# A block with attention mixers and experts on one core: the input laid out by features as well, and the first weight column loaded in halves

## The reference

```python
def first_block(x, norm_mix, w_in, ...):
    h = rms_norm(x, norm_mix[l])          # x * rsqrt(mean(x*x) + EPS) * norm_mix
    proj = h @ w_in[l]                    # 1024 -> 2974 columns
    qkv_a, z_a, b_a, a_a, q_b, kv_b, gate_b, u_c = split_columns(proj)
    y_a = gdn_mixer(...)                  # causal conv of qkv_a, gated delta rule
    y_b = nsa_mixer(...)                  # compressed, selected and window attention
    y_c = pool_mixer(...)
    x = x + concatenate([y_a, y_b, y_c]) @ w_out[l]
    h = rms_norm(x, norm_ffn[l])
    x = x + square(relu(h @ w_ffn1[l])) @ w_ffn2[l]
```

## Time and profile before

| | |
|---|---|
| median of three runs | 1006.93 us |
| profiled execution, its time | 1007.91 us |
| profiled execution, its span from first to last instruction | 1006.1 us |
| mean granted clock of TensorE | 0.99 of 2.4 GHz |
| PE busy | 967.6 us, 96% of the span |
| DVE busy | 417.2 us, 41% |
| ACT busy | 192.1 us, 19% |
| POOL busy | 30.2 us, 3% |
| moved by DMA | 301.45 MB, 300 GB/s over the span |

### The profile page before, as it was taken

How to read it: one execution, slowest core, us unless ns; L and a number is a source line. 1 busy time by engine, 2 the same in 40 slices (tenths; PEclk the granted TensorE clock), 3 DMA queues, 4 the chain that set the end, 5 groups by cost and what they waited for, 6 DMA issues and landing times.

```text
span 1006.1 us, 15621 instructions
## 1 busy us (share of the span) xinstructions
PE 967.6 (96%) x6471; PEld 537.4 (53%) x6471; DVE 417.2 (41%) x807; ACT 192.1 (19%) x436; POOL 30.2 (3%) x92
## 2 busy tenths in 40 slices
PE   8999999999999999999999999999979898899997
PEld 8788876576666665568864533333323232332332
DVE  4566475275555555302223643722212222222214
ACT  3424344110000001214342200111101101011112
POOL 8200000000000000000000000000000000000000
PEclk9999999999999999999999999999999999999999
DMA  8436002775666689562245999999999999999995
GB/s 347 194 135 207 3 2 95 302 293 226 281 282 279 280 344 396 207 252 84 84 168 199 325 420 427 426 426 427 426 426 428 427 427 427 427 426 427 416 415 202
DMA packets 32338, 301.45 MB, mean 300 GB/s; under 512 B 6160, under 2 KB 6288, under 8 KB 14736
## 3 DMA queue, kind: packets, MB, share of 16 engines
q1 hardware_dynamic: 32128, 300.23, 73.0%
q10 hardware_dynamic: 144, 0.26, 0.1%
HBM read 299.43 MB, written 1.05 MB: 299 GB/s over the span
## 4 chain that ended last, share of the span: by engine, by line
PE 80%; DMA 10%; SPq 6%; issue 2%; DVE 1%; ACT 1%; ACTq 0%; DVEq 0%
PE PS L2098 12%; PE PS L1740 11%; PE PS L1339 10%; PE PS L1334 9%; PE PS L1789 8%; DMA slot<-in_moe_w_up_dram 8%; PE PS L2117 7%; SPq L722 6%; PE PS L2071 3%; PE PS L1567 2%; PE PS L1688 2%; DMA slot<-in_moe_w_down_dram 2%; PE PS L1783 1%; PE PS L2046 1%; PE PS L1925 1%
## 5 line engine op out<-in xcount | busy, mean ns | idle before, releaser
L1740 PE MATMUL PS<-XH,slot 128*128 128x256 f32 x512 | 113.3, 379 | 1.7 <-DVE XH L2672 0.9
L1740 PEld LDWEIGHTS PS<-XH,slot 128*128 128x128 f32 x512 | 97.1, 190 | 21.3 <-issue 8.9
L1334 PE MATMUL PS<-XH,slot 128*128 128x256 f32 x432 | 97.8, 383 | 1.0 <-DMA slot<-in_w_in_dram 1.0
L1334 PEld LDWEIGHTS PS<-XH,slot 128*128 128x128 f32 x432 | 80.7, 190 | 13.6 <-DMA slot<-in_w_in_dram 1.2
L2117 PE MATMUL PS<-slot,ATT 128*32 128x512 f32 x576 | 67.4, 616 | 7.9 <-DMA slot<-in_moe_w_up_dram 7.9
L2098 PE MATMUL PS<-slot,ATT 128*32 128x512 f32 x544 | 66.1, 604 | 8.9 <-issue 5.6
L1339 PE MATMUL PS<-slot,XH 128*128 128x256 f32 (+4 forms) x224 | 72.2, 477 | 0.0
L2098 PE MATMUL PS<-slot,MASKS 128*32 128x512 f32 x576 | 64.1, 594 | 1.4 <-DMA slot<-in_moe_w_down_dram 1.2
L2721 DVE SCALAR_TENSOR_TENSOR AR<-AR 128x384 f32<-128x384 f32 (+1 forms) x112 | 59.9, 613 | 0.0
L2071 PE MATMUL PS<-AR,DIAG 128*128 128x512 f32 x120 | 57.6, 605 | 0.0
L1339 PEld LDWEIGHTS PS<-slot,XH 128*128 128x128 f32 x224 | 41.8, 190 | 26.3 <-issue 15.5
(11 more groups left out here) (489 smaller groups left out, 1211.1 us busy)
## 6 DMA issues: line engine op xcount, KB each, us to landing
slot<-in_w_ffn_dram SPq DMA_DIRECT2D x16, 2048.0 KB, 8.3
slot<-in_moe_w_gate_dram SPq DMA_DIRECT2D x16, 2048.0 KB, 33.2
slot<-in_moe_w_down_dram SPq DMA_DIRECT2D x16, 2048.0 KB, 33.4
slot<-in_moe_w_up_dram SPq DMA_DIRECT2D x14, 2048.0 KB, 30.4
AR<-in_ada_w_dram SPq DMA_DIRECT2D x16, 1536.0 KB, 14.2
AR<-in_moe_w_gate_dram SPq DMA_DIRECT2D x9, 2048.0 KB, 25.6
AR<-in_moe_w_up_dram SPq DMA_DIRECT2D x8, 2048.0 KB, 34.0
AR<-in_moe_w_down_dram SPq DMA_DIRECT2D x7, 2048.0 KB, 31.7
```

Of the source, the lines that this page charges most:

```text
L1334: ins = pe.matmul(dst, w[:, c * width + col:c * width + col + n], HT[:, c, :], start=(c == 0), stop=(c == KC - 1))
L1740: ins = pe.matmul(PS[:, b, (f % 2) * T:(f % 2 + 1) * T], slots[s][:, c * 512 + f * P:c * 512 + (f + 1) * P], HT[:, c, :], start=(c == 0), ...
```

## The change

The host gives x a second time, as `x_turned`: two halves of four feature chunks each, each row of a partition 4 KB. SP loads COL first, then the first half straight into HT, the lower half of weight column 0 (256 KB), the second half of x_turned (512 KB), the upper half of column 0, and column 1; only then the two row tiles of x, and columns 2 and 3. DVE scales HT in place, chunk by chunk (`x_scaled`), with its waits on the two halves. The transposes, their four groups and ACT's two copies are gone; twelve identity products (`wake`) stand in place of eight. The product of column 0 waits for each chunk and for each half of the column. `root_rows` moves from behind column 0 into the middle of column 2. Four semaphores for roots become one that is counted up (`norms_ready`), and `z_gated` becomes a step of DVE's own counter.

```diff
-    g = [(f"norm0_{b}", "DDDA"[b]) for b in range(4)] + [("root_rows", "A")]
+    g = [("qkv0", "D"), ("root_rows", "A"), ("qkv1", "D"), ("qkv2", "D")]
-    g += [(f"qkv{b}", "D") for b in range(3)] + [("bq0", "A"), ("bq1", "A"), ("kw0", "A")]
+    g += [("bq0", "A"), ("bq1", "A"), ("kw0", "A")]
...
+            def turned_x(h):
+                sp.dma_start(HT[:, 4 * h:4 * h + 4, :].rearrange("p c t -> p (c t)"), a["x_turned"][h]).then_inc(sems[f"xt_loaded{h}"], 16)
+
+            def in_column(j, lo, hi, done):
+                col = a["w_in"][j * P * D:(j + 1) * P * D].rearrange("(p n) -> p n", p=P)
+                sp.dma_start(slots[0][:, j * D + lo:j * D + hi], col[:, lo:hi]).then_inc(sems[done], 16)
+
+            sp.dma_start(COL[:, 0:COLS], a["cols"]).then_inc(sems["cols_loaded"], 16)
+            turned_x(0)
+            in_column(0, 0, D // 2, "in0_low")
+            turned_x(1)
+            in_column(0, D // 2, D, "in0_column0")
+            in_column(1, 0, D, "in0_column1")
             for i in range(NT):
                 sp.dma_start(XR[:, i, :], a["x"][0, i * P:(i + 1) * P, :]).then_inc(sems[f"x_loaded{i}"], 16)
-            sp.dma_start(COL[:, 0:COLS], a["cols"]).then_inc(sems["cols_loaded"], 16)
...
+            in_column(2, 0, D, "in0_column2")
+            in_column(3, 0, D, "loaded0")
...
-                    if i == 1:
-                        bank_ = wait_filled(act, "norm0_3")
-                        act.wait_ge(sems["cols_loaded"], 16)
-                        for c in (6, 7):
-                            ins = act.activation(HT[:, c, :], bank_[:, (c % 2) * T:(c % 2 + 1) * T], ACT.Copy, scale=COL[:, R_MIX + c:R_MIX + c + 1])
-                        ins.then_inc(sems["emptied_by_act"], 1)
...
-            rsqrt(RN, N2, 1.0, RNL, sems["qk_rnorm"])
+            rsqrt(RN, N2, 1.0, RNL, sems["norms_ready"])
...
-            def first_transposes():
+            def wake():
                 pe.wait_ge(sems["const_ready"], 1)
-                for k in range(8):
-                    pe.matmul(bank("norm0_3")[:, 0:P], IDENT[:, :], IDENT[:, :], start=True, stop=True)
-                for i in range(NT):
-                    pe.wait_ge(sems[f"x_loaded{i}"], 16)
-                    for b4 in range(4):
...
+                for k in range(12):
+                    pe.matmul(bank("bq0")[:, 0:P], IDENT[:, :], IDENT[:, :], start=True, stop=True)
...
-            def channel_major(dst, w, width, col, n=P, first=False):
+            def channel_major(dst, w, width, col, n=P, first=False, roots=False):
 
                 for c in range(KC):
-                    if first and c % 2 == 0:
-                        wait_emptied(pe, f"norm0_{c // 2}")
+                    if first:
+                        pe.wait_ge(sems["x_scaled"], c + 1)
+                        if c % 4 == 0:
+                            pe.wait_ge(sems["in0_column0" if c else "in0_low"], 16)
+                    if roots and c == 4:
+                        root_rows()
...
-                        ins = channel_major(dst, w[:, j * D:(j + 1) * D], P, 0, first=(j == 0))
-                        if j == 0:
-                            root_rows()
+                        ins = channel_major(dst, w[:, j * D:(j + 1) * D], P, 0, first=(j == 0), roots=(j == 2))
...
-                for b4 in range(3):
-                    b = wait_filled(dve, f"norm0_{b4}")
-                    for c in (2 * b4, 2 * b4 + 1):
-                        ins = ts(HT[:, c, :], b[:, (c % 2) * T:(c % 2 + 1) * T], gain[:, c:c + 1], None, ALU.mult)
-                    ins.then_inc(freed, 1)
+                for c in range(KC):
+                    dve.wait_ge(sems[f"xt_loaded{c // 4}"], 16)
+                    ts(HT[:, c, :], HT[:, c, :], gain[:, c:c + 1], None, ALU.mult).then_inc(sems["x_scaled"], 1)
```

More of the change, by code:

```diff
@@ L359, in build @@
             "xn_ready", "counts_ready", "recip_ready", "sig_exp", "conv_ready", "conv_exp", "silu_ready",
-            "qk_rnorm", "qk_ready", "hid_exp", "hid_ready", "nqk_rnorm", "nqk_ready",
-            "kc_rnorm", "kc_ready", "cmax", "cexp", "smax", "sexp", "probs_ready",
+            "norms_ready", "qk_ready", "hid_exp", "hid_ready", "nqk_ready",
+            "kc_ready", "cmax", "cexp", "smax", "sexp", "probs_ready",
             "dt_parts", "g_ready", "decay_exp", "egc_ready", "lt_ready", "pm_ready", "rhs_ready",
-            "kde_in", "z_gated", "o_rnorm", "ya_ready", "stored", "x_half", "ffn_bank_done", "shift_filled", "shift_taken", "qk_filled", "qk_taken", "rw_scaled", "ffn_hid_filled", "ffn_out_done",
+            "kde_in", "ya_ready", "stored", "x_half", "ffn_bank_done", "shift_filled", "shift_taken", "qk_filled", "qk_taken", "rw_scaled", "ffn_hid_filled", "ffn_out_done",
             "ffn_relu", "ffn_act_ready", "ada_used0", "ada_used1", "ada_loaded0", "ada_loaded1", "ada_step",
@@ L532, in load @@
                 fill(s, src)
+            def turned_x(h):
[9 more added lines that the diff above has]
+            in_column(1, 0, D, "in0_column1")
             for i in range(NT):
                 sp.dma_start(XR[:, i, :], a["x"][0, i * P:(i + 1) * P, :]).then_inc(sems[f"x_loaded{i}"], 16)
-            sp.dma_start(COL[:, 0:COLS], a["cols"]).then_inc(sems["cols_loaded"], 16)
[L537 to L541, removed]
+            in_column(2, 0, D, "in0_column2")
+            in_column(3, 0, D, "loaded0")
+            in_at = 4 * P * D
             for u, (c0, w) in enumerate(IN_UNITS):
@@ L1052, in _ @@
                     act.wait_ge(sems["nqk_ready"], 1)
-                    rsqrt(MR, M2, 1.0 / HD, N2[:, 0:20], sems["nqk_rnorm"])
+                    rsqrt(MR, M2, 1.0 / HD, N2[:, 0:20], sems["norms_ready"])
                 if lv == 4:
@@ L1075, in _ @@
             act.wait_ge(sems["kc_ready"], 1)
-            rsqrt(KN2[0:30, 1:2], KN2[0:30, 0:1], 1.0 / HD, LNV[0:30, 0:1], sems["kc_rnorm"])
+            rsqrt(KN2[0:30, 1:2], KN2[0:30, 0:1], 1.0 / HD, LNV[0:30, 0:1], sems["norms_ready"])
             for j in range(2):
@@ L1088, in _ @@
             act.wait_ge(sems["ya_ready"], 1)
-            rsqrt(OR, O2, 1.0 / HD, M2[:, 0:12], sems["o_rnorm"])
+            rsqrt(OR, O2, 1.0 / HD, M2[:, 0:12], sems["norms_ready"])
             nsa_output(0)
@@ L1347, in channels @@
                     if j < 4:
-                        if j < 3:
+                        if 0 < j < 3:
                             pe.wait_ge(sems[f"in0_column{j}"], 16)
-                            w = slots[0]
-                        else:
-                            w = weights("in0")
-                        ins = channel_major(dst, w[:, j * D:(j + 1) * D], P, 0, first=(j == 0))
-                        if j == 0:
-                            root_rows()
+                        w = slots[0] if j < 3 else weights("in0")
+                        ins = channel_major(dst, w[:, j * D:(j + 1) * D], P, 0, first=(j == 0), roots=(j == 2))
                     else:
@@ L2447, in _ @@
             tt(KDE, GLS, GCS[:, 0:6], ALU.subtract).then_inc(sems["kde_in"], 1)
-            dve.wait_ge(sems["qk_rnorm"], 1)
+            dve.wait_ge(sems["norms_ready"], 1)
             rn = RN.rearrange("p (i h) -> p i h", i=NT)
@@ L2546, in nsa_probs @@
                 tt(PR[i][t][:, :, 0:w], PR[i][t][:, :, 0:w], bc(sm_, 2, w), ALU.mult).then_inc(sems["probs_ready"], 1)
+            z_gated = []
             def gate_z(i):
                 dve.wait_ge(sems["sig_exp"], 3 + i)
-                tt(SIG[:, i, 0:GW], SIG[:, i, 0:GW], SG[:, i, 0:GW], ALU.mult).then_inc(sems["z_gated"], 1)
+                z_gated.append(step.begin(tt(SIG[:, i, 0:GW], SIG[:, i, 0:GW], SG[:, i, 0:GW], ALU.mult)))
             dve.wait_ge(sems["const_ready"], 6)
@@ L2574, in _ @@
             level(3)
-            dve.wait_ge(sems["nqk_rnorm"], 1)
+            dve.wait_ge(sems["norms_ready"], 2)
             tt(nq, nq, bc(MR, 2, HD), ALU.mult).then_inc(sems["nqk_ready"], 1)
@@ L2611, in _ @@
             dve.tensor_copy(SST[:, :, :], b[:, 0:3 * HD].rearrange("p (j d) -> p j d", d=HD)).then_inc(freed, 1)
-            dve.wait_ge(sems["kc_rnorm"], 1)
+            dve.wait_ge(sems["norms_ready"], 3)
             ts(KCN[0:30, :], KCN[0:30, :], KN2[0:30, 1:2], None, ALU.mult).then_inc(sems["kc_ready"], 1)
@@ L2652, in _ @@
             gate_z(1)
-            dve.wait_ge(sems["o_rnorm"], 1)
+            dve.wait_ge(sems["norms_ready"], 4)
             step(tt(oo, oo, bc(OR, 2, HD), ALU.mult))
-            dve.wait_ge(sems["z_gated"], NT)
+            step.until(z_gated[-1])
             for i in range(NT):
@@ L3188, in _ @@
             finish_right(1)
-NAMES = ["x", "cols", "pbc", "w_in", "cmp_w1", "cmp_w2", "pool_w", "w_out", "w_ffn1", "w_ffn2", "ada_w_2", "ada_b_2",
+NAMES = ["x", "x_turned", "cols", "pbc", "w_in", "cmp_w1", "cmp_w2", "pool_w", "w_out", "w_ffn1", "w_ffn2", "ada_w_2", "ada_b_2",
          "sb_w_in_2", "sb_w_out_2", "moe_w_grp_2", "moe_w_exp_2", "moe_w_gate_2", "moe_w_up_2", "moe_w_down_2"]
@@ L3218 @@
```

(2 more changed lines are left out.)

11 lines of the change are left out of this document (2 added, 9 removed).

## The result

The changed kernel took 1010.74 us as the median of 20 runs (1007.91 to 1013.03), the kernel before 1007.87 us beside it (20 runs, 1005.58 to 1010.53). The ratio is 1.0026, 95% interval [1.0018, 1.0035]: slower by a quarter of a per cent, some 2.6 us, close to the forecast of 2.8 (the medians lie 2.87 us apart). The forecast was laid on a median of 1006.93 us for before, and the kernel before measured here is 0.9 us slower than that: on the forecast's own base the ratio gives 1009.5 us, against 1009.7; the raw 1010.74 lies 0.14 above the top of its range. The profiled execution of after took 1011.43 us with a span of 1009.6.

A forecast was written before the change was run, and what follows sets the result against it. PE running without a gap behind the 8.5 us load of column 0 was taken as the bound; column stage -1.85, in3 +3.15, clock +1.5, together +2.8 on the median 1006.93: 1009.7 us, range 1004.9 to 1010.6.

The forecast's parts named there:

- column stage: Weight columns 0 to 5 ahead of bq0: ends at 28.1 us against 29.96, a gain of 1.85 us.
- in3: Load read first by bq0: 1.05 MB more ahead costs 2.7 us, landing at 31.1; bq0 starts 1.3 us later.
- pause: PE between column 5 and bq0: ready at 28.1 us, waits 3.0 us for in3.
- clock: Behind the pause before bq0: a likely fall of PE's clock, priced at 1.5 us, bounds nothing to 1.9.
- Start and column 0: First stage: identity products end at 6.4 to 6.9 us, column 0's upper half lands at 8.5, column 0 ends at 10.3.
- Rival (e): Column 0 starts at 8.5 us or later, HT scaled late: 1 us more, hidden by in3, no total changed; no chance given.
- The roots: Root product in the middle of column 2: diagonal ready at 14.4 us, product at 15.5.
- The cover: Roots ready 1.1 us before their product in column 2; without that margin PE would stop there.
- Columns 1 to 5: Columns at 3.45 us each, column 2 and in1 landing in time, column 5 ending at 28.1 us.
- Rival (b): Loads at 12.3 to 17.2 us: queue finds room, pause near 2 us, clock holds; +0.2, 1007.1 us, chance 0.15.
- Rival (a): At bq0: the wait for in3 comes but the clock holds; +1.3, 1008.2 us, chance 0.23.
- Carried one to one: From the first stage to the end: a shift at 30 us counts in full, since the experts' refills move with PE.

The follow-up runs named there:

- experiment 6: The changed kernel with input loads in order in1, in3, in5, in2, in4, in6, and GpSimd's table building held until DVE has scaled x: 1006.67 us, 0.9992.
- e2: The kernel before with input loads in the order in1, in3, in5, in2, in4, in6: 1007.50 us, ratio 0.9999.
- e4: The kernel before with x loaded a second time, read by nobody, ahead of in1: 1010.1 us, ratio 1.0013.
- e11: The kernel before with the load of out0 held back until PE has filled P51, near 110 us: 1005.71 us, ratio 0.9978.
- e12: The changed kernel, unchanged, profiled a second time: 1007.71 us.
- e13: The changed kernel, unchanged, profiled a third time: 1011.82 us.
- e8: The changed kernel with the load of out0 held back until PE has filled P51: 1007.93 us, ratio 1.0005.
- e3: The changed kernel with eight identity products nobody reads ahead of bq0, filling most of the pause: 1010.2 us, ratio 1.0017.
- e1: The changed kernel with input loads in the order in1, in3, in5, in2, in4, in6: 1006.65 us, ratio 0.9990.
- e10: The changed kernel with the new input order, GpSimd held until x is scaled, and out0 held back: 1004.44 us, ratio 0.9967.

## Why the prediction came true, step by step

The path was right: column stage, in3, pause, clock. That the sum was this close (2.8 forecast, 2.6 measured) is luck in part. The columns gained 1 us less than forecast, which the wait for in3 hid; the clock was counted in full and falls only in part of the executions, while bq0 starts somewhat later than forecast in the mean.

*Start and column 0.* The twelve identity products end at 6.04 us (forecast: 6.4 to 6.9). PE's first product of column 0 starts at 6.29 us (forecast: before 7). The upper half of the column landed at 8.7 (8.5). But column 0 ends near 11.25 us (16.42, less the column and a half of 3.45 us behind it), not at 10.3. The term that was off is the scaling, taken as 0.43 us a chunk from two instructions at 16.99 us; it took 0.63, because GpSimd builds its tables at that time (experiment 6). Rival (e) had named this: chunk 7 was ready at 10.65 instead of 9.1, it cost 1 us, and in3 hid it. With GpSimd silent the forecast of the stage fits: columns done at 16.07 + 12.25 = 28.3, against 28.1.

*The roots.* The product stands at 16.42 instead of 15.5. Not because the roots came late: DVE's second diagonal is done at 15.2, and PE arrives at 16.42. The cover held, and the shift is that of column 0.

*Columns 1 to 5.* No pause: column 2, column 3 and in1 came in time, as worked out. The columns end at 16.85 + 12.25 = 29.1, so the gain is 0.85 us and not 1.85. It varies: before's columns end at 29.4 to 29.96 us in the traces of before, e2, e4 and e11, after's at 29.1 in after, e12, e13 and e8, so the gain is 0.3 to 0.9 us.

*in3.* It was to land at 31.1 and landed at 31.07 (10.47 + 20.60). bq0 started 1.31 us later than before, forecast 1.3. The pause is 2.0 and not 3.0 because the columns took 1 us more: both errors are the same microsecond, and a wait that ends with a DMA swallows it. Rival (b) asked whether the hole of the earlier trace rows would close. It moved. From 12.3 to 17.2 us the rate is 451 GB/s instead of 346, from 17.2 to 23.9 it is 342, where before had 400. Over the 11.6 us that is 4.50 MB against 4.38, and the next stretch gives it back (404 against 431 GB/s over 4.5 us). So the megabyte cost its full price: 2.67 us in after, near the 2.7 that was taken and below the 3.1 of the lower rate, and 3.0 us in e4. The pieces cost no rate: from 8.5 to 12.3 us, among loads of 256 and 512 KB, after has 416 GB/s.

*The clock.* Forecast 1.5 us, within 0 to 1.9. When the clock falls it costs 1.7 to 1.8; but it fell in two of the three profiled executions of after and held in that of e8, whose loading is the same up to there. The step "I take the fall as likely" should have been a price times a frequency; that PE comes back at half rate each time, as the prediction quotes, isn't so here. With these four traces (bq0 at 31.11, 30.86, 31.86 and 31.02, against 29.80 before: +1.4 in the mean; the fall in two of four: +0.9) the sum is an estimated +2.3 us; the timed runs gave +2.6. Before's own start varies too (29.80, 29.67 in e2, 29.28 in e11), and by their mean the same sum is +2.5. The spread of the runs doesn't tell the two outcomes apart: after's covers 5.1 us (1007.91 to 1013.03), before's 5.0. Rival (a) was thus no rival but the other part of the same kernel's executions.

*Carried one to one.* +3.11 us at 47 us, no step back at 600. In e12, where the clock held, the product just ahead of the experts starts 1.2 us later than in before (597.55), with bq0 1.06 later. The end of the experts gave back 0.8 us; from the end of that product to the end of the span the fourteen traces take 397.9 to 399.6 us, so this lies in that part's own spread.

*What I hadn't seen.* The "issue" pause near 100 us, in both kernels alike. It doesn't enter the difference measurably (1.0026 with it, 1.0027 without), but it is worth 1.5 to 2.2 us to either, nearly as much as the whole change.

## What to carry to other kernels

In this kernel bytes added ahead of a queue's later loads were paid by the first reader that has no reserve: so before moving a load forward, list for each later load when it lands and when it is first read, and reorder by first use. An early stage that gets faster in front of such a reader buys only a longer pause, and a pause of PE has a second price in its clock, to be counted as a price times how often it falls. A bulk load that is issued long before it is needed wasn't free either: look for "issue" pauses on PE beside it.

## What the runs showed of the hardware that I had not expected

- Pauses of PE of like length may or may not be followed by the 1.2 GHz level (a granted clock of 0.50): behind pauses for in3 it fell at 2.01 and 2.72 us and held at 1.71, 1.85 and 1.91; behind the "issue" pause it fell at 2.22 (e3) and held at 2.32 (after) and 2.22 (e1). Near 560 us it fell in e10, e11 and e13 with no pause ahead of it. Length alone doesn't decide; what else does stays open.
- Beside a 2048 KB load PE stops for 1.2 to 2.3 us in the middle of a run of 64x64 products that read none of it, at a fixed place in its list of instructions and 1.2 to 1.5 us behind a packet of the queue "instruction" (nine traces), and not at all when the load is issued 15 to 18 us later (five traces).
- DVE's tensor_scalar of 128x256 float32 takes 0.285 us alone and 0.63 us (shares of a run of them) beside GpSimd's memsets and selects.
- A stretch of lower DMA rate among the 512 KB and 2 MB loads (346 GB/s at 12.3 to 17.2 us before, 219 to 299 from 18 to 21 us after) moves with the queue. What it is wasn't tried.
